# Turning attention probabilities and rotated queries and keys in 32 x 32 blocks on VectorE instead of whole tiles on TensorE, in a two-layer hybrid trunk

## The reference

```
h = rms_norm(x, g_pre_mix)
(a_u, a_v, b_q, b_k, b_v, c_b, c_c, c_x, d_cq, d_ckv, d_kr, gate_logits) = split_columns(h @ w_in)
out_a = chunked_sgu(gelu(a_u), gelu(a_v), ...)
out_b = moba_attention(partial_rope(b_q), partial_rope(b_k), b_v)       # 4 heads of 64, softmax
out_c = short_conv_mixer(c_b, c_c, c_x, c_w_conv)
out_d = mla_attention(d_cq, d_ckv, d_kr, ...)                           # 4 heads, 64 + 32 rotated
gates = sigmoid(gate_logits)
merged = sum_i gates[:, :, i] * (branches[i] @ w_branch[i])
x = x + rms_norm(merged @ w_out, g_post_mix)
x = x + rms_norm(square(relu(rms_norm(x) @ w_mlp_in)) @ w_mlp_out, g_post_mlp)
```

## Time and profile before

| | before |
|---|---|
| median of 3 runs | 791.03 us (790.62 to 791.67) |
| span of the profiled execution, first to last instruction | 788.9 us |
| TensorE busy | 781.6 us (99%) |
| VectorE busy | 506.3 us (64%) |
| ScalarE busy | 407.6 us (52%) |
| mean rate of the transfers | 185 GB/s |
| mean granted clock of TensorE | 0.999 |

### The profile page before, as it was taken

How to read it: one execution, slowest core, us unless ns; L and a number is a source line. 1 busy time by engine, 2 the same in 40 slices (tenths; PEclk the granted TensorE clock), 3 DMA queues, 4 the chain that set the end, 5 groups by cost and what they waited for, 6 DMA issues and landing times.

```text
span 788.9 us, 11019 instructions
## 1 busy us (share of the span) xinstructions
PE 781.6 (99%) x4053; PEld 659.3 (84%) x4053; DVE 506.3 (64%) x706; ACT 407.6 (52%) x631; POOL 62.3 (8%) x86
## 2 busy tenths in 40 slices
PE   9999999999999999999999999999999999999997
PEld 6898778888888888888889987878888888888885
DVE  5677655559777556555666876554788856565663
ACT  7566656443575445443546575554436745444441
POOL 1210000006110000000020100000333000000000
PEclk9999999999999999999999999999999999999999
DMA  9696555554466656567826855555654675656531
GB/s 310 187 304 190 160 161 157 176 202 133 149 198 216 209 178 190 191 188 220 275 66 199 281 162 160 158 163 187 186 157 140 200 225 185 187 185 207 179 119 53
DMA packets 88200, 145.86 MB, mean 185 GB/s; under 512 B 10316, under 2 KB 51556, under 8 KB 88164
## 3 DMA queue, kind: packets, MB, share of 16 engines
q1 hardware_dynamic: 88020, 145.24, 59.3%
q10 hardware_dynamic: 144, 0.13, 0.1%
HBM read 144.31 MB, written 1.05 MB: 184 GB/s over the span
## 4 chain that ended last, share of the span: by engine, by line
PE 99%; DVE 0%; POOL 0%; ACT 0%; POOLq 0%; issue 0%; DVEq 0%
PE banks L1352 24%; PE banks L1354 24%; PE banks L1353 24%; PE banks L1400 11%; PE banks L1401 5%; PE banks L1404 2%; PE banks L1585 1%; PE banks L1448 1%; PE banks L1466 1%; PE banks L1403 1%; PE banks L1364 1%; PE banks L1440 1%; PE banks L1410 1%; PE banks L1372 0%; PE banks L1438 0%; PE banks L1518 0%
## 5 line engine op out<-in xcount | busy, mean ns | idle before, releaser
L860 DVE TENSOR_TENSOR w_lo<-raw,w_hi 128x1024 fp32r<-128x1024 f32 (+1 forms) x256 | 306.3, 1225 | 123.8 <-ACT w_hi L529 123.4
L529 ACT CAST w_hi<-raw 128x1024 fp32r<-128x1024 f32 (+1 forms) x256 | 257.0, 1041 | 107.5 <-PE banks L1404 46.3
L1352 PE MATMUL banks<-w_hi,xT_both 128*128 128x512 f32 (+2 forms) x472 | 183.1, 388 | 0.0
L1354 PE MATMUL banks<-w_hi,xT_both 128*128 128x512 f32 (+2 forms) x472 | 178.6, 378 | 0.0
L1353 PE MATMUL banks<-w_lo,xT_both 128*128 128x512 f32 (+2 forms) x472 | 178.4, 378 | 0.0
L1400 PE MATMUL banks<-xT_both,w_hi 128*128 128x512 f32 x364 | 130.4, 398 | 0.0
L1352 PE MATMUL banks<-w_hi,brT_hi 128*128 128x512 f32 x320 | 125.4, 392 | 0.0
L1354 PE MATMUL banks<-w_hi,brT_lo 128*128 128x512 f32 x320 | 124.7, 390 | 0.0
L1353 PE MATMUL banks<-w_lo,brT_hi 128*128 128x512 f32 x320 | 124.7, 390 | 0.0
L1352 PEld LDWEIGHTS banks<-w_hi,xT_both 128*128 128x128 f32 x472 | 88.8, 188 | 18.6 <-issue 1.7
L1354 PEld LDWEIGHTS banks<-w_hi,xT_both 128*128 128x128 f32 x472 | 88.7, 188 | 16.4
(11 more groups left out here) (202 smaller groups left out, 757.0 us busy)
## 6 DMA issues: line engine op xcount, KB each, us to landing
raw<-in_w_in_dram SPq DMA_DIRECT2D x88, 512.0 KB, 4.6
raw<-in_w_mlp_in_dram SPq DMA_DIRECT2D x64, 512.0 KB, 4.7
raw<-in_w_mlp_out_dram SPq DMA_DIRECT2D x64, 512.0 KB, 4.3
raw<-in_w_branch_dram SPq DMA_DIRECT2D x16, 512.0 KB, 4.3
raw<-in_w_out_dram SPq DMA_DIRECT2D x16, 512.0 KB, 3.5
gate_th<-in_w_in_dram SPq DMA_DIRECT2D x8, 512.0 KB, 8.5
raw<-in_w_in_dram SPq DMA_DIRECT2D x8, 352.0 KB, 6.5
x<-in_x_dram SPq DMA_DIRECT2D x4, 256.0 KB, 4.2
```

The costliest lines, as they stand in the source:

```text
L529: nc.scalar.copy(w_hi[:, c % RING, h * n:(h + 1) * n], raw_of(q)[:, 0:n]).then_inc(hi_ready, 1)
L860: v.tensor_tensor(w_lo[:, c % RING, cut], raw_of(q)[:, 0:n], w_hi[:, c % RING, cut].bitcast(F32), ALU.subtract).then_inc(lo_ready, 1)
L1352: nc.tensor.matmul(dst, l_hi, r_hi, start=first, stop=False)
L1354: return nc.tensor.matmul(dst, l_lo, r_hi, start=False, stop=last)
```

## The change

1. The 24 transposes of probabilities per layer leave TensorE, and so do ScalarE's copies of them. VectorE turns a pair's probabilities straight from `probs` to `probsT` by 16 instructions, each for one of the 4 x 4 blocks of 32 x 32, over 32 partitions and six such blocks (`pair_transpose`). They stand in pieces of 5, 5 and 6 behind the splits of three steps.
2. The same for the rotated q and k of branch B: 16 block transposes per layer, four behind the splits of steps 7 to 10 (`qk_transpose`), for eight transposes on TensorE and two copies on ScalarE.
3. Pairs come every fourth chunk: scores after 13, 17, 21 and 25, values after 17, 21, 25, and those of the last pair after unit 3 (`LAST_VALUES_AFTER`). Both heads of a pair are masked, and exponentiated, in one step; the division moves to ScalarE (`pair_normalise`), one step later.
4. The transposes of branch D's rotated parts move from chunk 12 to chunk 15, their copies from step 13 to step 16. The spatial product moves from chunk 14 to 17.
5. The last pair's result goes to bank 2 instead of 5, its rounding (`branch_hi`, `branch_lo`) behind the gate chunks, and units wait for branch B's input at the start and for branch D's only in its own units.

```diff
             SQUARES += [(l + 1, "x", 0, 0), (l, "y", 1, 1)] if l + 1 < L else [(l, "y", 1, 1)]
         TAIL = 3
+        SCORES_AFTER = (13, 17, 21, 25)
+        VALUES_AFTER = (17, 21, 25)
+        LAST_VALUES_AFTER = 3
+        BLOCKS = [(a, b) for a in range(4) for b in range(4)]
...
+            def pair_exp(l, p):
+                for h in (2 * p, 2 * p + 1):
+                    for t in range(T):
+                        act.wait_ge(scores_masked, nth(l, 16, 2 * h + t))
...
+            def pair_normalise(l, p):
+
+                act.wait_ge(inv_sum_ready, nth(l, 4, p))
+                for h in (2 * p, 2 * p + 1):
+                    for t in range(T):
+                        part = probs[:, h % 2, 0:P] if t == 0 else probs[:, h % 2, P:3 * P]
+                        last = nc.scalar.activation(part, part, ACT.Copy,
+                                                    scale=inv_sum[:, h // 4, t, h % 4:h % 4 + 1])
+                last.then_inc(probs_normed, 1)
...
-                    for n, dst in enumerate((qTB, kTB)):
-                        act.wait_ge(qkTB_psum, nth(l, 2, n))
-                        nc.scalar.copy(dst.rearrange("p f n -> p (f n)"), psum[:, 6 + n, :]).then_inc(qkTB_copied, 1)
...
-                if s == 13:
+                if s == 16:
                     act.wait_ge(ropeT_psum, nth(l, 2, 0))
...
-                if 15 <= s < 23:
-                    head_copy(l, s - 15)
-                if 14 <= s < 22:
-                    head_exp(l, s - 14)
...
+                if s - 1 in SCORES_AFTER:
+                    pair_exp(l, SCORES_AFTER.index(s - 1))
+                if s - 2 in SCORES_AFTER:
+                    pair_normalise(l, SCORES_AFTER.index(s - 2))
+                if s == 19:
                     act.wait_ge(a_out_ready, nth(l, 1, 0))
...
-                if s in (19, 23):
-                    n = (s - 19) // 4
-                    act.wait_ge(attn_psum, nth(l, 4, 2 * n + 1))
-                    branch_hi(l, (1, 3)[n], psum[:, (3, 5)[n], :])
+                if s - 1 == VALUES_AFTER[1]:
+                    act.wait_ge(attn_psum, nth(l, 4, 1))
+                    branch_hi(l, 1, psum[:, 3, :])
...
+                act.wait_ge(attn_psum, nth(l, 4, 3))
+                branch_hi(l, 3, psum[:, 2, :])
...
+            def pair_inverse(l, p):
+
+                dve.wait_ge(probs_ready, nth(l, 16, 4 * p + 3))
+                n = 2 * (p % 2)
+                v.reciprocal(inv_sum[:, p // 2, :, n:n + 2], row_sum[:, p // 2, :, n:n + 2]
+                             ).then_inc(inv_sum_ready, 1)
+
+            def pair_transpose(l, p, blocks):
+
+                if blocks[0] == BLOCKS[0]:
+                    dve.wait_ge(probs_normed, nth(l, 4, p))
+                    if p >= 1:
+                        dve.wait_ge(attn_psum, nth(l, 4, p - 1))
+                flat = "p h (c n) -> p (h c) n"
+                for a, b in blocks:
+                    last = v.transpose(probsT[32 * b:32 * b + 32].rearrange(flat, n=P)[:, :, 32 * a:32 * a + 32],
+                                       probs[32 * a:32 * a + 32].rearrange(flat, n=P)[:, :, 32 * b:32 * b + 32])
+                if blocks[-1] == BLOCKS[-1]:
+                    last.then_inc(probsT_ready, 1)
+
+            def qk_transpose(l, blocks):
+
+                if blocks[0] == BLOCKS[0]:
+                    dve.wait_ge(ropeB_ready, nth(l, 1, 0))
+                    if l > 0:
+                        dve.wait_ge(attn_psum, nth(l - 1, 4, 1))
+                for a, b in blocks:
+                    rows_a, rows_b = slice(32 * a, 32 * a + 32), slice(32 * b, 32 * b + 32)
+                    last = v.transpose(
+                        qkTB[rows_b].rearrange("p n f (t c) -> p t (n f) c", t=T)[:, :, :, rows_a],
+                        proj[rows_a, :, MIX:3 * MIX].rearrange("p t (g c) -> p t g c", c=P)[:, :, :, rows_b])
+                if blocks[-1] == BLOCKS[-1]:
+                    last.then_inc(qkTB_ready, 1)
...
-                if 14 <= s < 22:
-                    head_mask(l, s - 14)
-                    head_normalise(l, s - 14)
-                if s == 15:
+                if s - 1 in SCORES_AFTER:
+                    p = SCORES_AFTER.index(s - 1)
+                    if (l, p) != (0, 0):
+                        dve.wait_ge(probsT_ready, nth(l, 4, p - 1))
+                    head_mask(l, 2 * p)
+                    head_mask(l, 2 * p + 1)
+                if s - 2 in SCORES_AFTER:
+                    pair_inverse(l, SCORES_AFTER.index(s - 2))
+                if s - 4 in SCORES_AFTER:
+                    pair_transpose(l, SCORES_AFTER.index(s - 4), BLOCKS[10:])
+                if s == 18:
                     dve.wait_ge(sv_psum, nth(l, 1, 0))
                     dve.wait_ge(u_gelu, nth(l, 1, 0))
...
-                if s == 16:
+                if s == 19:
                     branch_lo(l, 0, ORDER_A, a_out)
-                if s in (19, 23):
-                    n = (s - 19) // 4
-                    branch_lo(l, (1, 3)[n], (ORDER_B, ORDER_D)[n], psum[:, (3, 5)[n], :])
+                if s - 1 == VALUES_AFTER[1]:
+                    branch_lo(l, 1, ORDER_B, psum[:, 3, :])
...
+                    elif s - 2 in SCORES_AFTER:
+
+                        side_step(l, s)
+                        split(l, s + 3)
+                        pair_transpose(l, SCORES_AFTER.index(s - 2), BLOCKS[:5])
+                    elif s - 3 in SCORES_AFTER:
+
+                        side_step(l, s)
+                        split(l, s + 3)
+                        pair_transpose(l, SCORES_AFTER.index(s - 3), BLOCKS[5:10])
                     else:
                         side_step(l, s)
                         split(l, s + 3)
-
-                for n in range(4):
-                    gate_unit(l, n)
+                    if 7 <= s < 11:
+                        qk_transpose(l, BLOCKS[4 * (s - 7):4 * (s - 6)])
+
+                gate_unit(l, 0)
+                pair_transpose(l, 3, BLOCKS[10:13])
+                gate_unit(l, 1)
+                pair_transpose(l, 3, BLOCKS[13:])
+                gate_unit(l, 2)
+                gate_unit(l, 3)
+                branch_lo(l, 3, ORDER_D, psum[:, 2, :])
...
-                    pe.wait_ge(qkTB_copied, nth(l, 2, 1))
+                    pe.wait_ge(qkTB_ready, nth(l, 1, 0))
...
-            def head_transpose(l, h):
-                pe.wait_ge(probs_normed, nth(l, 16, 2 * h + 1))
-                if h >= 1:
-                    pe.wait_ge(probsT_copied, nth(l, 8, h - 1))
-                for b in range(3):
-                    last = nc.tensor.transpose(psum[:, 2, b * P:(b + 1) * P], probs[:, h % 2, b * P:(b + 1) * P],
-                                               ident)
-                last.then_inc(probsT_psum, 1)
...
-                pe.wait_ge(probsT_copied, nth(l, 8, 2 * p + 1))
+                pe.wait_ge(probsT_ready, nth(l, 4, p))
...
-                bank = psum[:, (3, 5)[p // 2], f * S:(f + 1) * S]
+                bank = psum[:, (3, 2)[p // 2], f * S:(f + 1) * S]
...
-                if c == 5:
-                    pe.wait_ge(ropeB_ready, nth(l, 1, 0))
-                    pe.wait_ge(wsT_copied, nth(l, 1, 0))
-                    for n in range(2):
...
-                                                           proj[:, t, o:o + P], ident)
-                        last.then_inc(qkTB_psum, 1)
...
-                    pe.wait_ge(qkTB_copied, nth(l, 2, 1))
+                    pe.wait_ge(wsT_copied, nth(l, 1, 0))
...
-                if c == 12:
+                if c == 15:
                     pe.wait_ge(ropeD_ready, nth(l, 2, 1))
...
-                if c == 14:
+                if c in SCORES_AFTER:
+                    pair_scores(l, SCORES_AFTER.index(c))
+                if c == 17:
...
-                if c in (16, 18, 20, 22):
-                    pair_values(l, (c - 16) // 2)
-                if 14 <= c < 22:
-                    head_transpose(l, c - 14)
-                if c in (13, 15, 17, 19):
-                    pair_scores(l, (c - 13) // 2)
+                if c in VALUES_AFTER:
+                    pair_values(l, VALUES_AFTER.index(c))
...
+                        pe.wait_ge(brT_lo_ready, nth(l, 4, ORDER_B))
+                    if i == NB - 1:
                         pe.wait_ge(brT_lo_ready, nth(l, 4, ORDER_D))
...
+                    if n == LAST_VALUES_AFTER:
+                        pair_values(l, 3)
```

More of the change, by code:

```diff
@@ L136, in hybrid_trunk @@
         vD = sb("vD", [P, T, HEADS * D_V])
-        qTB = sb("qTB", [P, FT, S])
-        kTB = sb("kTB", [P, FT, S])
+        qkTB = sb("qkTB", [P, 2, FT, S])
+        qTB, kTB = qkTB[:, 0], qkTB[:, 1]
         qTD = sb("qTD", [P, HEADS, S])
@@ L213, in hybrid_trunk @@
         ropeB_ready = sem("ropeB_ready")
-        qkTB_psum = sem("qkTB_psum")
-        qkTB_copied = sem("qkTB_copied")
+        qkTB_ready = sem("qkTB_ready")
         av_squared = sem("av_squared")
@@ L603, in merged_hi @@
```

(33 more changed lines are left out.)

6 lines of the change are left out of this document (1 added, 5 removed).

## The result

The changed kernel takes 802.79 us (median of 5 runs, 801.31 to 804.04) against 790.99 us of before (790.62 to 791.67): ratio 1.0148, 95% interval 1.0136 to 1.0160, slower by 1.5%. I had forecast 790.8 us, no change. The profiled execution has a span of 801.2 us, 12.3 more than before.

What follows compares the result with a forecast made beforehand. The prediction took TensorE to bound the kernel: -7.4 us from its shorter list, +6.2 for the last pair's waits and +1.0 for tanh waits, so 791.03 - 0.2 = 790.8 us, range 787.6 to 795.3.

Steps and rivals of the forecast that it cites:

- What bounds the kernel: Whole kernel: TensorE, busy 99% of the span and 99% of the chain; other engines' work is free unless TensorE waits.
- TensorE's shorter list: Both layers: transposes that leave TensorE and gathered small work shorten its list by 7.4 us (6.6 to 8.2).
- gathering small work: Spatial product and three of four value groups directly behind scores: fewer changes of matmul kind save 0.4 us per layer.
- The wait of the last pair: After unit 3: TensorE waits 11p - 0.2, or 3.1 us per layer, for eleven block transposes of p us each on VectorE.
- p = 0.30: VectorE's time in us for one block transpose of 192 elements; bounds 0.20 and 0.47.
- The clock behind it: Behind the last pair's waits: TensorE runs at half speed, 2.5 us each, 795.8 us after both; chance 0.19.
- q and k cost nothing: Steps 7 to 10: sixteen blocks per layer, 1.3 us in each of four steps on VectorE, costed at nothing.
- the 0.15 us in chunk 14: Chunk 14: two more exponentials ahead of the second tanh make TensorE wait 0.15 us for it in each layer.
- the wait in chunk 16: Chunk 16: copies ahead of the second tanh make TensorE wait 0.35 us for it in each layer.
- a split in steps 7 to 12 that TensorE waits for: Sign that the forecast is wrong: q and k blocks delay such a split.
- my -0.2: Forecast change in us: -7.4 for TensorE's list, +6.2 for the last pair's waits, +1.0 for waits for a tanh.
- The pairs in between: Gate chunks: block transposes of earlier pairs are hidden, so TensorE doesn't wait at the values after chunks 17, 21 and 25.

Runs made afterwards that it cites:

- experiments 4: The changed kernel with both tanh of a gate group at the start of ScalarE's step: 796.54 us, ratio to before 1.0065.
- 7: The changed kernel with the last pair one chunk earlier and both tanh at the start of ScalarE's step: 785.55 us, ratio to before 0.9935.
- Experiment 2: The changed kernel with 40 unused transposes on TensorE just ahead of the wait for the last pair's probabilities: 799.66 us, ratio to before 1.0101.
- Experiments 3: The changed kernel with q and k of branch B turned by TensorE and copied by ScalarE again: 800.78 us, ratio to before 1.0122.
- 5: The kernel before, with only q and k of branch B turned in blocks by VectorE in steps 7 to 10: 794.13 us, ratio 1.0038.

## Why the prediction was wrong

**What bounds the kernel, and TensorE's shorter list: right.** With hardly a wait in them the gate chunks take 96.7 us (experiments 4 and 7), 3.65 less than before; 1.05 of that is values that moved among the units (20.4 to 21.45). The net is 2.6 per layer. My 2.45 for the probabilities' transposes explains nearly all of it; the other 0.15 I put down to gathering small work, where I had 0.4, by what is left and not by a run. For q and k, the first gate product comes 0.6 us earlier in layer 0, and the way from the merged rows of layer 0 to the gate chunks of layer 1 is 0.9 shorter. TensorE's list is thus shorter by 2 x 2.6 + 1.5 = 6.7 us; I had 7.4, with 6.6 as the lower bound.

**The wait of the last pair: mechanism right, its size off.** I had said that eleven blocks stand on the way and that TensorE waits 11p - 0.2. With p = 0.38 that is 4.0, and 4.26 was measured. I took p = 0.30, near what 192 elements cost in a row of ordinary instructions. The duration of 0.37 is near what ordinary instructions would give (0.28 for 128 elements and 0.69 for 512 make 0.35 for 192), but block transposes don't overlap each other. The gatings between them took 0.72 from start to start, for which I had 0.6. Two layers idle for 8.5 us, where I had 6.2.

**The clock behind it: a rival, at 0.19, and true.** Experiment 2 shows that it is the idle time that lowers it. It cost 2.7 and 1.4 us, where I had worked out 2.5 each. I priced the rivals one at a time, and this one came together with p = 0.38. By my own terms the two together are 791.03 - 7.4 + 8.0 + 1.0 + 5.0 = 797.6 us, and the 5 us up to the measured time are beyond both. The twin of this rival, low clock behind the wait of 2 us, I had not thought of, since I had no such wait.

**q and k cost nothing: this step failed**, and with it the 0.15 us in chunk 14. I wrote that the blocks stood "well ahead of the scores after chunk 13" and costed them "at nothing for the same reason", that is, by the reserve that VectorE has in the gate chunks. But the blocks stand in steps 7 to 10, and the gate chunks begin at 12. These are the pauses of VectorE in the kernel before, from there to the first gate chunks, and the end of branch A's polynomial:

```profile
54.24 1.23 DVE L860 TENSOR_TENSOR w_lo<-raw,w_hi 128x1024 fp32r<-128x1024 f32 x1 [0.58 <-ACT w_hi L529]
56.94 1.22 DVE L860 TENSOR_TENSOR w_lo<-raw,w_hi 128x1024 fp32r<-128x1024 f32 x1 [1.48 <-ACT w_hi L529]
58.94 2.54 DVE L860 TENSOR_TENSOR w_lo<-raw,w_hi 128x1024 fp32r<-128x1024 f32 x2 [0.78 <-ACT w_hi L529]
...
66.91 2.36 DVE L860 TENSOR_TENSOR w_lo<-raw,w_hi 128x1024 fp32r<-128x1024 f32 x2 [0.88 <-ACT w_hi L529]
...
71.84 0.69 DVE L1079 TENSOR_TENSOR gate_th<-gate_th,banks 128x512 f32<-128x512 f32 x1
```

They add up to 3.7 us (the same four in layer 1 to 2.9), where the blocks take 7.1, so everything behind them moved: the polynomial's end starts at 76.30 for 71.84. I asked when the blocks' own result is needed, and not what stands behind them in VectorE's list: branch A's polynomial, for which ScalarE waited ahead of the exponentials and the tanh. Experiments 3 and 4 show the chain from both ends, and 5 shows without the pairing that the blocks make VectorE late, though TensorE met that at another place. Against experiment 3 the blocks cost 2.0 us in the gate chunks of layer 0 (99.07 less 97.05) and 3.6 in layer 1, with the low clock. With the wait in chunk 16, which I had predicted, it is 2.4 (99.07 less 96.66) and 4.0. What I had named as a sign, a split in steps 7 to 12 that TensorE waits for, didn't come: the chain went by the polynomial, the mask and the tanh.

**The sum again, with what was measured:** -6.7 for TensorE's list; +8.7 for the last pair (25.8 less 21.45, twice); +4.1 for the clock behind it (28.47 less 25.81, 27.24 less 25.80); +6.4 in the gate chunks for the tanh and the clock behind it. That is 12.5, and 801.2 less 788.9 is 12.3. Against my -0.2 that is 12.7 more: 5.4 in the gate chunks, 4.1 for the clock, 2.5 for the last pair's wait and 0.7 for TensorE's list. The split inside the units rests on experiment 2, whose filler is about as long as the wait that it fills.

**The pairs in between** were covered, as predicted: no wait for the values after chunks 17, 21 and 25 in any trace. In chunk 16 of the changed kernel TensorE waited 0.27 us in each layer, where I had predicted 0.35.

## What to carry to other kernels

When work goes to an engine that isn't the bound, ask what stands behind it in that engine's list and who waits for that, at each place it is put; a reserve measured in one stage says nothing of the next. A result that the bounding engine needs (here a tanh) belongs ahead of everything on its engine that waits for a third one. And a wait of the matrix engine can cost more than its length (4.26 us of it were followed by 2.7 or 1.4 us of low clock): move the work that causes it, since the same instructions with the last pair one chunk and one tanh some instructions earlier went from 1.5% slower to 0.65% faster than before.

## What the runs showed of the hardware

- Block transposes of 32 partitions in fp32 took 370 ns for 192 elements and 436 for 256, and came 0.38 and 0.445 us apart, without overlap, where elementwise instructions of 0.28 us came 0.20 apart. The Trainium skill (VectorE: DVE Perf Modes, The three transpose paths) gives 311 ns for 128 x 128 in bf16, which is sixteen blocks of 32 x 32; the instruction here, in fp32, handled six or eight blocks, all read from one group of 32 partitions, in more time than that.
- A wait of 4.26 us was followed by the low clock in both layers, until 5.5 us after the wait in one (177.46 to 182.94) and 2.9 after it in the other (572.61 to 575.54, the last products 0.43 apart). Waits of 4.25 to 4.26 us at the same place in experiments 3 and 4 also left one layer's units at 28.3 or 28.5 us and the other's at 27.3 or 27.4. Of two waits of 1.96 and 1.95 in the changed kernel only the second was followed by the low clock. It began late: products came 0.23 apart from 479.27 to 480.21, behind the wait that ended at 478.93, and then 0.43 apart until 483.60.
- 40 transposes in a row kept the granted clock at 1.00 through 4.4 us without a product.
